# Routing one-hots of a product-key mixer: compare and gate in one vector operation per token, all differences of the second key on GpSimd

## What is computed

```python
q = (t @ w_q).reshape(T, PEER_HEADS, 2, PEER_HALF)
s = jnp.einsum('thpd,hpnd->thpn', q, sub_keys)
s_top, i_top = lax.top_k(s, PEER_TOPK)          # 16 best of each half
...
ids = ...                                       # i * 128 + j, 8 heads x 16 = 128 experts a token
gates = jax.nn.softmax(best_s, axis=-1)
act = jax.nn.gelu(jnp.einsum('td,ted->te', x_c, u[ids_c]), approximate=False)
return jnp.einsum('te,ted->td', g_c * act, v[ids_c])
```

## Time and profile before

| what | us |
|---|---|
| timed runs, three, median (range) | 1158.25 (1155.82 to 1158.5) |
| span of the profiled execution | 1152.3 |
| routing stage in it, 669.88 to 797.11 | 127.2 |
| DVE / PE / ACT / POOL busy in the whole span | 786.0 / 1085.2 / 621.2 / 120.7 |

### The profile page before, as it was taken

The page is one execution under the profiler, slowest core; times in us unless marked ns, Lnnn a source line. Parts: engine busy times, 40 slices in busy tenths (PEclk is TensorE's granted clock), DMA queues, the critical chain, the costliest instruction groups (busy, mean ns, idle before and its releaser), DMA issues.

```text
span 1152.3 us, 20363 instructions
## 1 busy us (share of the span) xinstructions
PE 1085.2 (94%) x7278; PEld 1002.3 (87%) x7278; DVE 786.0 (68%) x1333; ACT 621.2 (54%) x1034; POOL 120.7 (10%) x101
## 2 busy tenths in 40 slices
PE   7999999989999999999999976667999999999998
PEld 6988999889899999999999975656888888888886
DVE  5774674453488889888884489998555555555554
ACT  6775555453555555555555576665545545455453
POOL 0000110010000000000000067884000000000000
PEclk9999999999999999999999988898999999999999
DMA  9544345252355454555445520001555555555552
GB/s 318 167 149 145 111 167 163 74 183 110 112 181 184 180 184 180 182 184 182 183 180 185 185 86 0 0 0 36 188 204 191 185 198 200 182 191 207 184 187 105
DMA packets 60658, 179.54 MB, mean 156 GB/s; under 512 B 4048, under 2 KB 42960, under 8 KB 44112
## 3 DMA queue, kind: packets, MB, share of 16 engines
q1 hardware_dynamic: 60624, 179.09, 44.7%
HBM read 178.03 MB, written 1.05 MB: 155 GB/s over the span
## 4 chain that ended last, share of the span: by engine, by line
PE 48%; issue 40%; DVE 7%; ACT 2%; POOL 2%; DMA 1%; DVEq 0%; POOLq 0%; SPq 0%; ACTq 0%
PE acc L1262 30%; PE acc L1044 13%; PE bank L1243 2%; DVE act_w L968 2%; DVE oh_i L957 2%; DVE oh_j L957 1%; POOL oh_i L320 1%; ACT wsp L347 1%; DVE wsp L663 1%; DMA wraw<-w_in 1%; PE bank L1148 0%; PE bank L1126 0%; POOL sqd L327 0%; PE bank L1073 0%; POOL wsp L312 0%
## 5 line engine op out<-in xcount | busy, mean ns | idle before, releaser
L886 DVE TENSOR_TENSOR hl<-raw,hl 128x1024 fp32r<-128x1024 f32 x192 | 234.4, 1225 | 170.0 <-ACT hl L577 168.2
L577 ACT ACTIVATE hl<-raw 128x1024 fp32r<-128x1024 f32 x192 | 202.6, 1056 | 135.7 <-PE acc L1262 126.3
L1262 PE MATMUL acc<-hl,whl 128*128 128x512 f32 x1152 | 266.6, 389 | 1.8 <-DVE whl L985 1.8
L1262 PEld LDWEIGHTS acc<-hl,whl 128*128 128x128 f32 x1152 | 216.3, 188 | 46.6 <-issue 1.9
L1214 PE MATMUL bank<-xt,hl 128*128 128x256 f32 x768 | 218.1, 284 | 0.0
L1215 PE MATMUL bank<-xt,hl 128*128 128x256 f32 x768 | 217.5, 283 | 0.0
L1216 PE MATMUL bank<-xt,hl 128*128 128x256 f32 x768 | 217.5, 283 | 0.0
L1214 PEld LDWEIGHTS bank<-xt,hl 128*128 128x128 f32 x768 | 147.5, 192 | 0.3 <-DVE hl L886 0.3
L1215 PEld LDWEIGHTS bank<-xt,hl 128*128 128x128 f32 x768 | 147.6, 192 | 0.2 <-issue 0.2
L1216 PEld LDWEIGHTS bank<-xt,hl 128*128 128x128 f32 x768 | 147.5, 192 | 0.0
L663 DVE TENSOR_TENSOR wsp<-wraw,wsp 128x2048 fp32r<-128x2048 f32 x35 | 80.2, 2290 | 73.9 <-ACT wsp L347 73.7
(11 more groups left out here) (207 smaller groups left out, 1448.3 us busy)
## 6 DMA issues: line engine op xcount, KB each, us to landing
raw<-u_t SPq DMA_DIRECT2D x64, 1024.0 KB, 4.8
raw<-v SPq DMA_DIRECT2D x64, 1024.0 KB, 4.7
wraw<-w_in SPq DMA_DIRECT2D x9, 1024.0 KB, 8.0
wraw<-w_pq SPq DMA_DIRECT2D x8, 1024.0 KB, 5.2
wraw<-w_ck SPq DMA_DIRECT2D x4, 1024.0 KB, 5.0
wraw<-w_cv SPq DMA_DIRECT2D x4, 1024.0 KB, 4.9
wraw<-w_out SPq DMA_DIRECT2D x4, 1024.0 KB, 4.9
wraw<-w_cq SPq DMA_DIRECT2D x4, 1024.0 KB, 5.0
```

The lines of the kernel that those rows point to most:

```text
L577: nc.scalar.activation(eslot(k, 0, second), raw[:, k // 2, k % 2], ACT.Copy).then_inc(ready, 1)
L886: V.tensor_tensor(eslot(k, 1, second), raw[:, k // 2, k % 2], eslot(k, 0, second).bitcast(F32), ALU.subtract).then_inc(ready, 1)
L1262: last = pe.matmul(acc[:, 2 * t + n], a, b[:, 512 * n:512 * n + 512], start=False, stop=last_key and k == 2, skip_group_check=True)
```

## The change

DVE now compares and gates in one tensor_scalar a token (128 columns, the first key and the gate as two per-partition scalars), four a group. POOL's gating pass and its semaphore are gone; POOL makes the differences of the second key for all four slots (a new tile `sqd3`). ACT squares and Relus all four slots, each in one operation of 512 columns. DVE makes no j one-hots. PE waits for two semaphores as before, of other names.

```diff
-            def gate_rows(g, t0, slot):
-                pool.wait_ge(s_oi, g + 1)
-                nc.gpsimd.tensor_tensor(oh_i(slot), oh_i(slot), kt3[:, 2, ds(t0, GRP)].unsqueeze(2).broadcast_to([P, GRP, P]),
-                                        ALU.mult).then_inc(s_gi, 1)
...
-            differences(0)
-            with pool.Fori(0, T // GRP // 4 - 1) as it:
+            differences(0, 0)
+            pool.wait_ge(s_um, KEYS)
+            for slot in range(1, 4):
+                differences(GRP * slot, slot)
+            with pool.Fori(1, T // GRP // 4) as it:
                 for slot in range(4):
-                    gate_rows(it * 4 + slot, it * (4 * GRP) + GRP * slot, slot)
-                    if slot == 1:
-                        differences(it * (4 * GRP) + 4 * GRP, it * 3 + 1)
...
+                    pool.wait_ge(s_oja, it * 4 + (slot - 3))
+                    differences(it * (4 * GRP) + GRP * slot, slot)
...
-            def onehots(it, n, g, t0, slot, first):
+            def onehot_j(g, slot, first):
+                act.wait_ge(s_dif, g + 1)
+                nc.scalar.activation(sqd(slot), sqd(slot), ACT.Square).then_inc(s_sqd, 1)
+                act.wait_ge(s_sqd, g + 1)
                 if not first:
                     act.wait_ge(s_gm, g - 3)
-                if slot == 0:
-                    act.wait_ge(s_dif, it + 1)
-                    last = nc.scalar.activation(sqd0[:], sqd0[:], ACT.Square)
-                for k in range(GRP if slot else 0):
-                    last = nc.scalar.activation(sqd(slot)[:, k], iota[:], ACT.Square, scale=-1.0, bias=kt3[:, 1, ds(t0 + k, 1)])
-                last.then_inc(s_sqd, 1)
-                act.wait_ge(s_sqd, n + 1)
                 nc.scalar.activation(oh_j(slot), sqd(slot), ACT.Relu, scale=-1.0, bias=ones[:, 0:1]).then_inc(s_oja, 1)
...
             def onehots(t0, slot):
-                equal(oh_i(slot), 0, t0).then_inc(s_oi, 1)
-                if slot == 3:
-                    equal(oh_j(slot), 1, t0).then_inc(s_ojd, 1)
+                for k in range(GRP):
+                    last = V.tensor_scalar(oh_i(slot)[:, k], iota[:], kt3[:, 0, ds(t0 + k, 1)], kt3[:, 2, ds(t0 + k, 1)],
+                                           ALU.is_equal, ALU.mult)
+                last.then_inc(s_oi, 1)
...
-                pe.wait_ge(s_gi, it * 4 + (slot + 1))
-                if slot == 3:
-                    pe.wait_ge(s_ojd, it + 1)
-                else:
-                    pe.wait_ge(s_oja, it * 3 + (slot + 1))
+                pe.wait_ge(s_oi, it * 4 + (slot + 1))
+                pe.wait_ge(s_oja, it * 4 + (slot + 1))
```

More of the change, by code:

```diff
@@ L82, in build @@
         gfin = at("gfin", 146 * K, [D])
+        sqd3 = at("sqd3", 150 * K, [GRP, P])
         sqd12 = at("sqd12", 140 * K, [2, GRP, P])
@@ L171, in build @@
         s_uh, s_ul, s_um, s_ua = (sem(n) for n in ("s_u_high", "s_u_low", "s_u_mm", "s_u_gelu"))
-        s_oi, s_gi, s_dif, s_ojd, s_oja, s_sqd, s_gm, s_gw = (sem(n) for n in (
-            "s_onehot_i", "s_gated_i", "s_differences", "s_onehot_j_dve", "s_onehot_j_act", "s_sq_distance", "s_route_mm", "s_route_mul"))
+        s_oi, s_dif, s_oja, s_sqd, s_gm, s_gw = (sem(n) for n in (
+            "s_onehot_i", "s_differences", "s_onehot_j_act", "s_sq_distance", "s_route_mm", "s_route_mul"))
         s_seed = sem("s_seed")
@@ L214, in sqd @@
         def sqd(slot):
-            return sqd12[:, slot - 1] if slot else sqd0[:]
+            return (sqd0[:], sqd12[:, 0], sqd12[:, 1], sqd3[:])[slot]
         def oh_i(slot):
@@ L316, in _, with differences @@
             pool.wait_ge(s_kte, 3)
-            def gate_rows(g, t0, slot):
-                pool.wait_ge(s_oi, g + 1)
-                nc.gpsimd.tensor_tensor(oh_i(slot), oh_i(slot), kt3[:, 2, ds(t0, GRP)].unsqueeze(2).broadcast_to([P, GRP, P]),
-                                        ALU.mult).then_inc(s_gi, 1)
[L323 to L327, removed]
-                                        iota[:].unsqueeze(1).broadcast_to([P, GRP, P]), ALU.subtract).then_inc(s_dif, 1)
-            differences(0)
-            with pool.Fori(0, T // GRP // 4 - 1) as it:
-                for slot in range(4):
-                    gate_rows(it * 4 + slot, it * (4 * GRP) + GRP * slot, slot)
-                    if slot == 1:
-                        differences(it * (4 * GRP) + 4 * GRP, it * 3 + 1)
-            for slot in range(4):
-                g = T // GRP - 4 + slot
-                gate_rows(g, GRP * g, slot)
+            def differences(t0, slot):
+                nc.gpsimd.tensor_tensor(sqd(slot), kt3[:, 1, ds(t0, GRP)].unsqueeze(2).broadcast_to([P, GRP, P]),
+                                        iota[:].unsqueeze(1).broadcast_to([P, GRP, P]), ALU.subtract).then_inc(s_dif, 1)
+            differences(0, 0)
[3 more added lines that the diff above has]
+            with pool.Fori(1, T // GRP // 4) as it:
+                for slot in range(4):
+                    pool.wait_ge(s_oja, it * 4 + (slot - 3))
+                    differences(it * (4 * GRP) + GRP * slot, slot)
         @block.scalar
@@ L607, in _ @@
                     nc.scalar.activation(kt3[:, jj - 4], bank[jj - 4][:, T:2 * T], ACT.Copy).then_inc(s_kte, 1)
-            def onehots(it, n, g, t0, slot, first):
+            def onehot_j(g, slot, first):
+                act.wait_ge(s_dif, g + 1)
+                nc.scalar.activation(sqd(slot), sqd(slot), ACT.Square).then_inc(s_sqd, 1)
+                act.wait_ge(s_sqd, g + 1)
                 if not first:
                     act.wait_ge(s_gm, g - 3)
-                if slot == 0:
-                    act.wait_ge(s_dif, it + 1)
-                    last = nc.scalar.activation(sqd0[:], sqd0[:], ACT.Square)
-                for k in range(GRP if slot else 0):
-                    last = nc.scalar.activation(sqd(slot)[:, k], iota[:], ACT.Square, scale=-1.0, bias=kt3[:, 1, ds(t0 + k, 1)])
-                last.then_inc(s_sqd, 1)
-                act.wait_ge(s_sqd, n + 1)
                 nc.scalar.activation(oh_j(slot), sqd(slot), ACT.Relu, scale=-1.0, bias=ones[:, 0:1]).then_inc(s_oja, 1)
-            act.wait_ge(s_kte, 3)
-            for slot in range(3):
-                onehots(0, slot, slot, GRP * slot, slot, True)
+            for slot in range(4):
+                onehot_j(slot, slot, True)
             with act.Fori(1, T // GRP // 4) as it:
-                for slot in range(3):
-                    onehots(it, it * 3 + slot, it * 4 + slot, it * (4 * GRP) + GRP * slot, slot, False)
+                for slot in range(4):
+                    onehot_j(it * 4 + slot, slot, False)
             def a_high(j, slot):
@@ L953, in _ @@
             dve.wait_ge(s_kte, 1)
-            def equal(dst, key, t0):
-                return V.tensor_tensor(dst, iota[:].unsqueeze(1).broadcast_to([P, GRP, P]),
-                                       kt3[:, key, ds(t0, GRP)].unsqueeze(2).broadcast_to([P, GRP, P]), ALU.is_equal)
             def onehots(t0, slot):
-                equal(oh_i(slot), 0, t0).then_inc(s_oi, 1)
-                if slot == 3:
-                    equal(oh_j(slot), 1, t0).then_inc(s_ojd, 1)
+                for k in range(GRP):
+                    last = V.tensor_scalar(oh_i(slot)[:, k], iota[:], kt3[:, 0, ds(t0 + k, 1)], kt3[:, 2, ds(t0 + k, 1)],
+                                           ALU.is_equal, ALU.mult)
+                last.then_inc(s_oi, 1)
             def weigh(g, t0, slot):
@@ L970, in _ @@
             for slot in range(4):
+                if slot == 0:
+                    dve.wait_ge(s_kte, 3)
                 if slot == 2:
-                    dve.wait_ge(s_kte, 3)
                     dve.wait_ge(s_um, KEYS)
```

## The result

The changed kernel takes 1170.26 us (median of 4 runs, 1165.74 to 1171.29) against 1158.38 before: ratio 1.010, 95% interval 1.0078 to 1.0122. It is slower by 12 us, and the prediction of 1170 holds.

A forecast was written before the change was run, and what follows sets the result against it. DVE was taken to bound the routing stage. 60 groups x (2.12 - 1.963) = +9.4 us and start +2.8 make +12: span 1152.3 to 1164.5, plus 5.9 for timed runs, 1170 us, range 1150 to 1181.

The forecast's parts named there:

- The turns: Claimed that DVE's tensor_scalars and POOL operations hold one shared SBUF port pair in turn, as 0.75 us stretched to 3.75.
- Part 1: DVE: removed one-hots 0.76 us a group, added four tensor_scalars at 0.24 each; alone 1.56 us against 1.963 now.
- Parts 2 and 5: POOL's 0.90 us hold against DVE's free 0.77 stops DVE 0.51 us a group; T = 1.56 + 0.13 + 2.45 - T = 2.07.
- p = 0.38: Time in us from a weighing's start to POOL's hold, from p = 2.45 - T.
- The chain of 2.45 us: Links from the end of a group's tensor_scalars through PE and ACT's Relu to POOL's hold, added up to 2.45 us.
- Part 6: Stage start: 16 tensor_scalars and POOL's turns before the first weighing, 9.2 us, 2.8 more than now.
- Parts 3 and 4: ACT needs 1.29 us a group, hidden under DVE; PE keeps 1.15 us and waits for the last of four tensor_scalars.
- The step from span to timed median: Timed runs taken as 5.9 us above the profiled span, so 1164.5 became 1170.
- A: Rival: two-pointer tensor_scalars use one port and need no turn; 1149 us (1140 to 1158), chance 0.13.
- C: Rival: cheap tensor_scalars, 0.13 us start to start; 1156 us, no difference; chance 0.12, with other ways to end at zero.
- D: Rival: turns always in the tensor_scalars, DVE stopped up to 0.83 us a group, T = 2.4; 1187 us, chance 0.06.
- B: Rival: POOL's turn falls under the weighing, DVE stopped only 0.13 us a group, T = 1.69; 1145 us, chance 0.11.

The follow-up runs named there:

- Experiment 1: Changed kernel with POOL's differences in the loop cut from 512 to 8 columns, all waits kept, so results are wrong: 1136.6 us.
- experiments 2 and 3: Changed kernel with POOL making differences for slot 0 alone (2) or slots 0 and 2 (3), ACT squaring the other slots: 1150.84 us and 1154.55 us.
- experiment 6: Kernel of Experiment 1 with the gate scalar of the tensor_scalars replaced by the constant 1: 1122.74 us.
- experiment 4: Changed kernel where POOL's difference also waits for the third tensor_scalar of the group four before: 1153.76 us.
- experiment 5: Changed kernel where POOL's difference also waits for the first tensor_scalar of the group four before: 1180.76 us.
- experiment 8: Kernel before with DVE's four gated tensor_scalars in place of one-hot and POOL gating, second key made as before: 1149.29 us.
- experiment 7: Changed kernel, POOL making differences for slots 0 and 2 only, each behind the third tensor_scalar of the group four before: 1143.61 us.

## Why the prediction was right

**The turns, right.** The prediction's step was that a tensor_scalar with one SBUF input takes turns with POOL. Experiment 1 takes the hold away, and DVE's 0.49 us of stop is gone in every group; experiments 2 and 3 lower it with the number of turns; 4 and 5 move it by place alone.

**Part 1, the price of a tensor_scalar: right within its bounds, a little too low.** Taken 0.24, measured 0.257; the upper bound of 0.27 (a second scalar costs as much as the first) is nearly it, by experiment 6. DVE's own need is 1.62 and not 1.56 us.

**Part 1 and the sum, a wrong comparison.** The prediction says that DVE's own work falls by 0.40 us a group and is eaten up by the turns. The 1.56 is a need without stops, the 1.963 beside it holds 0.60 of stops. By the prediction's own rows the need before was 1.36 (5.4 us a pass), so DVE's own work rises, by 0.20 as put and 0.26 as measured, and the time lost in turns falls. The forecast did not suffer, since it added up the new period from its parts, but its closing reason has the two terms the wrong way round.

**Parts 2 and 5, the stop: right in size, by a mechanism that is too regular.** Predicted 0.51 us a group, measured 0.49, or 0.54 over the 54 groups in which POOL takes part. But the argument had one steady place (p = 0.38) and one steady stop, while in the trace the place wanders: a POOL operation that starts just before a weighing leaves a group of some 1.75 us, one that starts among the tensor_scalars makes it 2.33 to 2.53. Hardly a group is stopped for 0.51. The chain of 2.45 us and the period don't lock; that PE's link changes with its clock may be one reason. That the mean agrees with the balance of chain and period is shown by this case only. With the measured 0.257 the prediction's own formula gives 2.10 at the full clock and 2.14 to 2.20 with the clock's share, and the 54 groups have 2.165. The 2.12 met the overall 2.111 in part by luck: t was put too low, and the six groups at 1.62 behind POOL's last difference were not thought of.

**Part 6, the start: direction right, size low.** The first weighing comes 10.8 us after the first one-hot, 9.2 were predicted (9.3 in experiment 4's kernel, where POOL is held back). Nine POOL operations follow each other there, all ahead of the first weighing, so eight behind the first one where six were counted:

```profile
672.15 9.52 POOL L320 TENSOR_TENSOR sqd<-kt,iota 128x512 f32<-128x512 f32 x9 [432.66 <-ACT kt L599]
```

The end, from the 61st weighing, was said to stay at 3.1 us and took 2.5 (810.13 to 812.60).

**Parts 3 and 4, right.** ACT's cycle at the start of the stage is 1.27 to 1.28 us a group, and ACT waits for PE 52.5 us in the stage; PE waits for DVE.

**The sum.** It is closer than its terms:

| term, us | predicted | measured |
|---|---|---|
| 60 groups | +9.4 | +8.9 |
| start | +2.8 | +4.4 |
| end | 0 | -0.6 |
| stage | +12.2 | +12.7 |

The step from span to timed median was wrong in kind: the 5.9 us were taken as lying around the span, but the changed kernel's profiled run has 1.8 (1171.21 against a span of 1169.4). The rest was the spread of the runs of the kernel before (1153.0 to 1160.2 over all that were timed): its profiled execution was among the shorter ones. The stage begins at 669.7 to 673.1 in the kernels of this study, in no order of their edits, so the changed kernel's later start (672.71) says nothing of the change. As both medians were compared, this cost nothing.

**The rivals.** A falls: undisturbed tensor_scalars of 0.33 us stand beside stopped ones, most of 1.06 to 1.23 us; the one under the POOL operation of 737.00 ends at 738.12, 0.08 after it. C falls by 0.257. D is what experiment 5 makes, at 2.30 us a group (2.4 had been put). B comes by itself in 15 of the 54 groups, at just its price (1.75 - 1.62 = 0.13), but not for good; with one wait every group comes near it, at 0.25.

## What to carry to other kernels

Where two engines take turns, count each operation of the one as a stop of the other, less what the other can do meanwhile without its turn; a pass moved from one such engine to the other is no saving by its busy time. Compare like with like: a new need without stops belongs beside the old need without stops. Look then for the instruction that needs no turn (here the weighing, with an operand in PSUM, which kept 0.68 us) and start the other engine's operation under it: that was worth 16.5 us of 1170 for one semaphore wait. And time the parts of a change apart, since here one half gained 9 us and the other lost more than twice that.

## What the runs showed of the hardware

- A tensor_scalar of 128 fp32 columns in SBUF starts the next one 0.196 us later with one per-partition scalar and 0.257 with two.
- A POOL tensor_tensor of 512 columns costs DVE 0.73 us where it starts among such tensor_scalars (experiment 5; 0.75 to 0.88 in experiment 2), 0.25 where it starts 0.06 us after a weighing with an operand in PSUM (experiment 4), and some 0.13 where it starts 0.08 to 0.12 us before one (experiment 8, and the 738.44 row of the changed kernel).
- A POOL tensor_tensor of 8 columns can be recorded with 1.10 us among tensor_scalars with two per-partition scalars, against 0.20 to 0.39 in other places of the same stage, and DVE's period stays at 1.62: its recorded length is not the time in which it stops DVE. In the kernel of experiment 6, with one scalar, none is over 0.34.
- PE's granted clock in the middle of the stage was 1.00 in the kernel of experiment 7, and over the stage 0.99 in that of experiment 4 and 0.79 in the changed kernel, with the same matmuls. In that of experiment 5 it was 0.68, and changed between 0.50 and 1.00, while the groups stayed at 2.34 to 2.35 us: there the clock did not set the pace. Why it differs between these kernels was not tried. The rows are of experiment 4, then 5:

```profile
669.89:793.48 123.59, 75.67 (x517) 63.76 (x515) 123.59 (x321) 86.38 (x129) 66.69 (x64) 0.99 0.04 13
680.00:800.00 120.00, 89.17 (x416) 77.02 (x414) 120.00 (x257) 66.23 (x104) 59.94 (x52) 0.68 0.00 0
```
